# Two input slabs of a hybrid decoder trunk as split fp32r products, with the split spread over ScalarE and VectorE

## The reference, cut to what matters

```python
h = layer_norm(x, ln_in_g, ln_in_b)                  # x: 1 x 256 x 1024, float32
for l in range(2):
    p = h @ w_in[l]                                  # 1024 x 2560
    q, k = rotary(p[q columns]), rotary(p[k columns])     # 8 heads x 64 each
    v = p[v columns]
    y_att = moba_attention(q, k, v)                  # one block of 256: plain causal attention here
    y_sg = gelu(u) * (W_s layer_norm(gelu(v_sg)) + b)     # u, v_sg: 256 columns each
    y_cv = silu(layer_norm(depthwise_conv_31(a * sigmoid(g))))   # a, g: 256 columns each
    h = layer_norm(alpha * h + concat(y_att, y_sg, y_cv) @ w_out[l])
    h = layer_norm(alpha * h + moe(h))               # router, top-1 group of 4, top-2 of its 4 experts
```

## Time and profile before

| | |
|---|---|
| median of 3 runs | 721.97 us (721.77 to 723.27) |
| profiled execution | 721.64 us, span 719.8 us |
| mean granted TensorE clock | 0.987 |
| TensorE matmul busy | 670.3 us (93%) |
| VectorE, ScalarE, GpSimd busy | 281.1, 141.3, 67.9 us |
| chain that ended last | PE 72%, DMA 18%, DVE 7% |
| fp32 slab matmuls in the chain (L465) | 15% |
| read from memory | 239.1 MB |

### The profile page before, as it was taken

How to read it: one execution, slowest core, us unless ns; L and a number is a source line. 1 busy time by engine, 2 the same in 40 slices (tenths; PEclk the granted TensorE clock), 3 DMA queues, 4 the chain that set the end, 5 groups by cost and what they waited for, 6 DMA issues and landing times.

```text
span 719.8 us, 7383 instructions
## 1 busy us (share of the span) xinstructions
PE 670.3 (93%) x3039; PEld 329.5 (46%) x3039; DVE 281.1 (39%) x585; ACT 141.3 (20%) x280; POOL 67.9 (9%) x65
## 2 busy tenths in 40 slices
PE   7999999999999999987689999989999999998882
PEld 4645587543333543332375446856333445332331
DVE  4496767410333022130627936771120330321226
ACT  3102453231110211110121026523201113100100
POOL 1603000410000000000050210006000000000001
PEclk9999999999999999999979999999999999999997
DMA  8999636099999999999999641433999999999991
GB/s 282 341 388 413 270 118 234 5 374 405 421 422 421 421 421 421 421 421 421 396 387 404 266 163 67 158 128 151 372 422 422 421 421 421 422 420 422 421 407 66
DMA packets 48572, 240.72 MB, mean 334 GB/s; under 512 B 4428, under 2 KB 8852, under 8 KB 23956
## 3 DMA queue, kind: packets, MB, share of 16 engines
q1 hardware_dynamic: 47956, 238.06, 82.4%
q10 hardware_dynamic: 576, 2.10, 0.7%
HBM read 239.10 MB, written 1.05 MB: 334 GB/s over the span
## 4 chain that ended last, share of the span: by engine, by line
PE 72%; DMA 18%; DVE 7%; issue 1%; ACT 1%; POOL 0%; DVEq 0%; POOLq 0%; ACTq 0%
PE bank L544 22%; PE bank L465 15%; PE bank L563 12%; DMA ring<-in_w_up 9%; DMA ring<-in_w_gate 8%; PE bank L479 5%; PE bank L522 5%; PE bank L625 4%; PE bank L583 3%; PE bank L552 1%; PE bank L443 1%; PE bank L697 1%; DVE stats L1217 1%; DVE h L1210 1%; PE bank L688 1%
## 5 line engine op out<-in xcount | busy, mean ns | idle before, releaser
L544 PE MATMUL bank<-ring,xe 128*64 128x512 f32 x1024 | 226.0, 594 | 14.9 <-DMA ring<-in_w_up 7.9
L544 PEld LDWEIGHTS bank<-ring,xe 128*64 128x64 f32 x1024 | 71.7, 137 | 162.4 <-issue 136.1
L563 PE MATMUL bank<-ring,area_b 128*64 128x512 f32 x512 | 113.4, 595 | 1.6 <-DVE area_b L1231 1.6
L465 PE MATMUL bank<-ring,xT_area 128*128 128x512 f32 x256 | 111.3, 593 | 0.0
L1225 DVE TENSOR_TENSOR area_b<-area_b,bank 128x512 f32<-128x512 f32 x16 | 11.0, 687 | 253.7 <-PE bank L544 253.7
L465 PEld LDWEIGHTS bank<-ring,xT_area 128*128 128x128 f32 x256 | 48.1, 190 | 57.4 <-issue 57.4
L563 PEld LDWEIGHTS bank<-ring,area_b 128*64 128x64 f32 x512 | 35.2, 137 | 68.4 <-issue 64.0
L950 POOL TENSOR_TENSOR rstd<-var_eps,half_neg 128x1 f32<-128x1 f32 x18 | 11.7, 660 | 544.9 <-DVE var_eps L1037 544.9
L1245 DVE SCALAR_TENSOR_TENSOR y_lo<-bank,slot_gate,y_hi 128x512 fp32r<-128x512 f32 x32 | 24.0, 751 | 89.2 <-ACT y_hi L871 89.2
L1293 DVE SCALAR_TENSOR_TENSOR mix<-glu,tapsT,mix 128x256 f32<-128x256 f32 x120 | 47.7, 471 | 0.0
L871 ACT ACTIVATE y_hi<-bank,slot_gate 128x512 fp32r<-128x512 f32 x32 | 22.0, 687 | 98.1 <-PE bank L563 98.1
(11 more groups left out here) (159 smaller groups left out, 577.2 us busy)
## 6 DMA issues: line engine op xcount, KB each, us to landing
ring<-in_w_gate SPq DMA_DIRECT2D x32, 2048.0 KB, 22.8
ring<-in_w_up SPq DMA_DIRECT2D x32, 2048.0 KB, 23.8
ring<-in_w_down SPq DMA_DIRECT2D x32, 2048.0 KB, 24.5
ring<-in_w_in SPq DMA_DIRECT2D x9, 2048.0 KB, 20.4
ring<-in_w_out SPq DMA_DIRECT2D x4, 2048.0 KB, 21.0
ring<-in_w_in SPq DMA_DIRECT2D x2, 1024.0 KB, 7.1
h<-in_x SPq DMA_DIRECT2D x2, 512.0 KB, 4.1
ln_par<-in_ln_mix_g ACTq DMA_DIRECT2D x2, 512.0 KB, 7.5
```

Of the source, the lines that this page charges most:

```text
L465: mm = pe.matmul(dst[:, :], xT[:, c, b * P:(b + 1) * P], w[:, c, :], start=c == 0, stop=c == KC - 1)
L544: mm = pe.matmul(bank[2 + u % 2][e * SLOTS:(e + 1) * SLOTS, :], xe[:, k, at + e * SLOTS:at + (e + 1) * SLOTS], w[:, e, c, :], start=k == 0 ...
L563: mm = pe.matmul(bank[5 + n][e * SLOTS:(e + 1) * SLOTS, :], hidT[:, k, e * SLOTS:(e + 1) * SLOTS], w[:, e, c, n * BANK:(n + 1) * BANK], st ...
```

## The change

The q and k slabs are computed like w_out: each chunk of 128 contraction rows and each row block is three fp32r matmuls. The turned input gets a high part (ScalarE, two copies of 1024 columns) and a low part (VectorE, four subtractions of 512). Each of the 16 weight chunks gets a high part in one of seven buffers (ScalarE) and a low part, which is written over the chunk in the ring (VectorE). Seven chunks are split ahead of the sigmoid (ScalarE) and of the gated product (VectorE); the others on ScalarE behind it as buffers come free, and on VectorE one after every second pair of taps.

On TensorE sgu moves ahead of the turn of the convolution's result, and the first block of v (now into bank 5) ahead of the turns of q and k. ScalarE takes over the copies of the turned k and of the set-up parameters; its silu moves behind the copies of turned q and k, and its load of the next layer norm's rows behind the last high part. The first layer norm's rows are loaded between the halves of slab 0, and GpSimd applies them before it masks the spatial weights.

```diff
+IN_SPLITS = 7
+IN_CHUNKS = 2 * KC
...
+        xi_hi = nc.alloc_sbuf_tensor_at("xi_hi", [P, KC, SEQ], F32R, offset=uv_at)
+        xi_lo = nc.alloc_sbuf_tensor_at("xi_lo", [P, KC, SEQ], F32R, offset=area_b_at + 4096)
+        in_hi_at = [uv_at + 8192 + 2048 * i for i in range(4)] + [area_b_at + 2048, area_a_at + 6144, area_a_at + 10240]
...
             def load_setup():
-                sp.dma_start(ln_par[:, 0, :], bcast_row(ln_in_g, D)).then_inc(par_in, 16)
-                sp.dma_start(ln_par[:, 1, :], bcast_row(ln_in_b, D)).then_inc(par_in, 16)
...
                     sp.dma_start(dst[:, :, CV:], src[:, :, CV:]).then_inc(first_half_in, 16)
+                    sp.dma_start(ln_par[:, 0, :], bcast_row(ln_in_g, D)).then_inc(par_in, 16)
+                    sp.dma_start(ln_par[:, 1, :], bcast_row(ln_in_b, D)).then_inc(par_in, 16)
                     sp.dma_start(dst[:, :, 0:CV], src[:, :, 0:CV]).then_inc(landed[0], 16)
...
+            def in_product(l, i, b):
+                n, c = i // KC, i % KC
+                if i == 0:
+                    pe.wait_ge(xi_hi_ready, TB * l + b + 1)
+                    pe.wait_ge(xi_lo_ready, TB * l + b + 1)
+                if b == 0:
+                    pe.wait_ge(in_lo_ready, IN_CHUNKS * l + i + 1)
+                w_hi, w_lo = in_hi[i % IN_SPLITS][:, :], in_lo[(l * LAYER_UNITS + 1 + n) % RING][:, c * BANK:(c + 1) * BANK]
+                for k, (x, w) in enumerate(((xi_hi, w_hi), (xi_lo, w_hi), (xi_hi, w_lo))):
+                    mm = pe.matmul(bank[2 * n + b][:, :], x[:, c, b * P:(b + 1) * P], w,
+                                   start=c == 0 and k == 0, stop=c == KC - 1 and k == 2)
+                    if b == TB - 1 and k == 1:
+                        mm.then_inc(in_chunk_used, 1)
+                if b == TB - 1 and c == KC - 1:
+                    mm.then_inc(used, 1)
...
-                rows_slab(u0 + 1, (0, 1))
-                if l == 0:
-                    pe.wait_ge(setup_copied, 1)
-                rows_slab(u0 + 2, (2, 3))
+                for i in range(IN_CHUNKS):
+                    if l == 0 and i == KC:
+                        pe.wait_ge(setup_copied, 1)
+                    for b in range(TB):
+                        in_product(l, i, b)
+                rows_slab(u0 + 3, (6, 7))
...
-                rows_slab(u0 + 3, (6, 7))
+                block_slab(u0 + 4, 0, bank[5]).then_inc(v0_pe, 1)
...
-                pe.wait_ge(conv_ln_done, TB * (l + 1))
-                block_slab(u0 + 4, 0, bank[4]).then_inc(v0_pe, 1)
...
+                pe.wait_ge(conv_ln_done, TB * (l + 1))
                 pe.wait_ge(v_ready, TB * l + 1)
...
+            def in_x_high(l):
+                for b in range(TB):
+                    act.wait_ge(tr_dve, TR_DVE * l + b + 1)
+                    act.wait_ge(tr_act, TR_ACT * l + b + 1)
+                    act.activation(xi_hi[:, :, b * P:(b + 1) * P], xT[:, :, b * P:(b + 1) * P], ACT.Copy)\
+                       .then_inc(xi_hi_ready, 1)
+            def in_w_high(l, i):
+                n = l * LAYER_UNITS + 1 + i // KC
+                if i % KC == 0:
+                    act.wait_ge(landed[n % RING], 16 * (n // RING + 1))
+                if i >= IN_SPLITS:
+                    act.wait_ge(in_chunk_used, IN_CHUNKS * l + i - IN_SPLITS + 1)
+                act.activation(in_hi[i % IN_SPLITS][:, :], unit_at(n)[:, i % KC * BANK:(i % KC + 1) * BANK], ACT.Copy)\
+                   .then_inc(in_hi_ready, 1)
...
                 scaled_columns(3 * l, 2 * l, [(0, 0), (1, 0)])
+                in_x_high(l)
+                for i in range(IN_SPLITS):
+                    in_w_high(l, i)
                 act.wait_ge(used, l * LAYER_UNITS + 1)
                 act.activation(conv_sig, bank[5][:, :].rearrange("p (c t) -> p c t", c=CB), ACT.Sigmoid)\
                    .then_inc(sig_ready, 1)
+                if l == 0:
+                    act.wait_ge(setup_pe, DEPTH + 1)
...
+                    ins.then_inc(setup_copied, 1)
+                for i in range(IN_SPLITS, IN_CHUNKS):
+                    in_w_high(l, i)
                 next_params(ln_mix_g[l], ln_mix_b[l], 2 * TB * l + TB)
+                act.wait_ge(used, l * LAYER_UNITS + 4)
...
+                for b in range(TB):
+                    for i in range(2):
+                        act.wait_ge(qkT_pe, 4 * l + 2 * b + i + 1)
...
                 act.wait_ge(conv_ln_done, TB * (l + 1))
                 act.activation(mix[:, :, ATT + SG:D], mix[:, :, ATT + SG:D], ACT.Silu).then_inc(conv_out, 1)
...
+            def in_x_low(l):
+                for b in range(TB):
+                    dve.wait_ge(xi_hi_ready, TB * l + b + 1)
+                    for half in range(2):
+                        x = slice(4 * half, 4 * half + 4), slice(b * P, (b + 1) * P)
+                        ins = dve.tensor_tensor(xi_lo[:, x[0], x[1]], xT[:, x[0], x[1]],
+                                                xi_hi[:, x[0], x[1]].bitcast(F32), ALU.subtract)
+                    ins.then_inc(xi_lo_ready, 1)
+            def in_w_low(l, i):
+                dve.wait_ge(in_hi_ready, IN_CHUNKS * l + i + 1)
+                at, cols = (l * LAYER_UNITS + 1 + i // KC) % RING, slice(i % KC * BANK, (i % KC + 1) * BANK)
+                dve.tensor_tensor(in_lo[at][:, cols], ring[:, at, cols], in_hi[i % IN_SPLITS][:, :].bitcast(F32),
+                                  ALU.subtract).then_inc(in_lo_ready, 1)
...
                 scaled_columns(3 * l, 2 * l)
+                in_x_low(l)
+                for i in range(IN_SPLITS):
+                    in_w_low(l, i)
...
                         ins.then_inc(conv_step, 1)
+                    if k % 2 == 1 and IN_SPLITS + k // 2 < IN_CHUNKS:
+                        in_w_low(l, IN_SPLITS + k // 2)
...
-                for b in range(TB):
-                    dve.wait_ge(qkT_pe, 4 * l + 2 * b + 2)
-                    dve.tensor_copy(qkT[:, 1, :, b * P:(b + 1) * P],
-                                    bank[2 + b][:, :].rearrange("p (c t) -> p c t", c=4)).then_inc(qkT_dve, 1)
```

More of the change, by code:

```diff
@@ L106, in trunk @@
         ring = sb("ring", [RING, UNIT])
+        ring_at = nc.sbuf_base - 4 * RING * UNIT
         h = sb("h", [TB, D])
@@ L190, in trunk @@
                    for i in range(SPLITS)]
+        xi_hi = nc.alloc_sbuf_tensor_at("xi_hi", [P, KC, SEQ], F32R, offset=uv_at)
+        xi_lo = nc.alloc_sbuf_tensor_at("xi_lo", [P, KC, SEQ], F32R, offset=area_b_at + 4096)
+        in_hi_at = [uv_at + 8192 + 2048 * i for i in range(4)] + [area_b_at + 2048, area_a_at + 6144, area_a_at + 10240]
+        in_hi = [nc.alloc_sbuf_tensor_at(f"in_hi{i}", [P, BANK], F32R, offset=at) for i, at in enumerate(in_hi_at)]
+        in_slots = sorted({(l * LAYER_UNITS + 1 + n) % RING for l in range(DEPTH) for n in range(2)})
+        in_lo = {at: nc.alloc_sbuf_tensor_at(f"in_lo{at}", [P, UNIT], F32R, offset=ring_at + 4 * UNIT * at) for at in in_slots}
         xe = nc.alloc_sbuf_tensor_at("xe", [P, KC, GROUP * P], F32, offset=xT_at)
@@ L253, in trunk @@
         proj_pe = sem("proj_pe")
+        xi_hi_ready = sem("xi_hi_ready")
+        xi_lo_ready = sem("xi_lo_ready")
+        in_hi_ready = sem("in_hi_ready")
+        in_lo_ready = sem("in_lo_ready")
+        in_chunk_used = sem("in_chunk_used")
+        taps_copied = sem("taps_copied")
         x_hi_ready = sem("x_hi_ready")
@@ L881, in _ @@
                    .then_inc(sig_ready, 1)
+                if l == 0:
+                    act.wait_ge(setup_pe, DEPTH + 1)
+                    nt = DEPTH * TAPS + DEPTH
+                    act.activation(tapsT[:, :, :], bank[3][:, 0:CB * nt].rearrange("p (c k) -> p c k", c=CB), ACT.Copy)\
+                       .then_inc(taps_copied, 1)
+                    act.activation(sgbT[:, :], bank[3][:, 256:256 + DEPTH * GROUPS], ACT.Copy)
+                    for n in range(DEPTH):
+                        ins = act.activation(sgwT[:, n, :, :], bank[6 + n][:, :].rearrange("p (g t) -> p g t", g=GROUPS),
+                                             ACT.Copy)
+                    ins.then_inc(setup_copied, 1)
+                for i in range(IN_SPLITS, IN_CHUNKS):
+                    in_w_high(l, i)
                 next_params(ln_mix_g[l], ln_mix_b[l], 2 * TB * l + TB)
-                act.wait_ge(conv_ln_done, TB * (l + 1))
-                act.activation(mix[:, :, ATT + SG:D], mix[:, :, ATT + SG:D], ACT.Silu).then_inc(conv_out, 1)
                 act.wait_ge(used, l * LAYER_UNITS + 4)
@@ L973, in gain_and_shift @@
                 pool.tensor_tensor(h[:, b, :], h[:, b, :], ln_par[:, 1, :], ALU.add).then_inc(h_ready, 1)
+            pool.wait_ge(norm_ready, TB)
+            for b in range(TB):
+                gain_and_shift(b, 0)
+            pool.wait_ge(setup_in, 16 * 4)
+            pool.affine_select(out=sgw_rows, in_=sgw_rows, compare_op=ALU.is_ge, fill=0.0, base=0,
+                               pattern=[[0, DEPTH * GROUPS], [-1, P]], channel_multiplier=1).then_inc(sgw_masked, 1)
```

43 lines of the change are left out of this document (16 added, 27 removed).

## The result

| | before | changed |
|---|---|---|
| median, first comparison (4 runs each) | 721.87 us (720.44 to 723.27) | 714.11 us (713.15 to 715.77) |
| ratio, first comparison | | 0.9895, 95% interval 0.987 to 0.9919 |
| median, second comparison (11 and 6 runs) | 721.85 us | 714.76 us |
| ratio, second comparison | | 0.9901, 95% interval 0.9881 to 0.9921 |
| profiled execution (its span) | 721.64 us (719.8) | 713.42 us (711.6) |

The change makes the kernel faster by 7.8 us by the first medians and 7.1 by the second. 714.3 was forecast, within 711.3 to 717.8.

The account below looks back on a forecast made before the run. The prediction took VectorE's period of 2.19 us per chunk to set the end of q and k. Gains of 2.7 and 5.1 less 0.2 us, 7.6 together, gave 714.3 us as a median, range 711.3 to 717.8.

Parts of the forecast that it names:

- TensorE's rate: In the q and k slabs: each fp32r matmul takes 0.227 us, 21.8 us for the 96.
- The last chunk: End of q and k: chunk 15's six matmuls take 1.36 us after a hand-over of 0.05 us.
- Layer 1: Layer 1's q and k products: done at 404.2 instead of 409.3 us, a gain of 5.1 us.
- Layer 0: Layer 0's q and k products: k lands at 35.0, done at 53.0 against 55.7 us, a gain of 2.7 us.
- What hides what: Both mixers: sgu and half of v hide taps and rotation, with 4.4 and 5.1 us of cover for the rotation.
- Exponentials, 1.1 us later, at no cost: ScalarE's exponentials: ready about 0.2 us before the spatial matmuls instead of 1.3, so 1.1 us later, costing nothing.
- The input's low parts: VectorE before the taps: four subtractions for the turned input, each costing 0.60 us.
- The first layer norm's rows: Layer 0's slab 0: loading them earlier delays its second half 2.7 us at most, at no cost to the sigmoid.
- The table load: ScalarE before layer 0's sigmoid: a load costs 1.28 us, against about 2.66 by the skill page.
- Rival (a): Both layers' q and k: TensorE's own rate decides, not VectorE's subtractions; 710.6 us, chance 8%.
- Rival (b): Layer 0: k lands no earlier or the sigmoid later, gain 0.8 us or below; 716.2 to 717 us, chance 18%.
- Rival (c): Both mixers: TensorE's waits lower its granted clock, slowing the sgu slab behind; 724.6 us, chance 5%.

Follow-up runs that it names:

- e1: Changed kernel with one subtraction after every pair of taps instead of every second pair: 710.32 us, ratio 0.9839 to the kernel before.
- e2: Changed kernel with the next layer norm's parameter rows loaded ahead of ScalarE's last nine high parts again: 718.79 us, one run.
- e8: Changed kernel with only the sigmoid's table loaded earlier, ahead of ScalarE's high parts: 717.59 us, one run.
- e3: Changed kernel with sgu put back behind the turns of conv and half of v behind those of q and k: 735.44 us, one run.
- e4: Changed kernel with only half of v put back behind the turns of q and k: 720.3 us, one run.
- e6: Changed kernel with subtractions late among the taps, then one after every pair, and the sigmoid's table loaded ahead of ScalarE's high parts: 711.09 us, ratio 0.984.
- e5: Changed kernel with GpSimd's gain and shift held back until VectorE's subtractions (layer 1: through chunk 6) are done: 716.45 us, one run.
- e7: e6 with 22 filler matmuls added ahead of layer 1's turns to keep the clock up: 716.23 us.

## Why the prediction was right, and where its terms were off

- **The bound.** Right. VectorE's period was forecast at 2.19 us and is 2.19; the chain shows it in both layers, and in e1 the bound is gone and q and k run at TensorE's rate.
- **TensorE's rate.** Right: 0.227 us a product, 21.79 for the 96 in e1.
- **The last chunk.** Mis-sized. 1.36 us were forecast; a chunk that begins after an idle moment takes 1.66, and its first matmul shows 0.50 us where the others show 0.40. The hand-over is 0.04 (0.05 forecast), but the subtraction behind VectorE's last wait counts with its 0.69 and not with 0.60. That is 0.4 us in each layer.
- **Layer 1.** q and k take 22.71 us against 27.47: 4.8 where 5.1 was forecast, for the reason above.
- **Layer 0.** The term that was mis-sized most: 2.7 us forecast, 1.3 to 1.7 measured. The mis-sized step is "1.05 MB at the 387 GB/s of a busy window are 2.7 us; I take three quarters of it, 2.0": k landed at 35.41 and 35.91 and not at 35.0. Counted from slab 0's start it lands at 23.1 us in both profiles, where it was 24.15, 24.19 and 24.27 in three of the kernel before: 1.0 to 1.2 us earlier. With the last chunk's 0.4 that is 1.2 to 1.4 us less. The lower bound of 0.8 with k at 36.9 was too high as well: e2, where k lands late, gains 0.35 at most. The mechanism was the right one: e2 moves k and the end of q and k by the same amount, and e8 moves the sigmoid by 1.35 us and the end of q and k not at all.
- **What hides what.** Right. e3 and e4 uncover it: the waits of 1.93 and 1.33 us in e4 are 6.87 us of half of v less the covers of 4.4 and 5.1 that were forecast, to within 0.5 and 0.4. The scores' wait for ScalarE's copies of the turned q and k costs 0.16 us a layer (0.1 forecast): in TensorE's timeline the sixteen turns take 1.91 us to the next matmul, and 1.75 in the kernel before.
- **Exponentials, 1.1 us later, at no cost.** They start at 80.69, 0.4 us ahead of the spatial product at 81.11 (0.2 forecast), so 0.8 later, and nothing behind them waits.
- **The input's low parts.** Mis-sized without a cost: 4 x 0.60 were taken, and beside GpSimd they took 6.81 and 6.56 us, ahead of the taps in both layers.
- **The first layer norm's rows.** Right. Slab 0 of layer 0 takes 14.05 us before and after, and GpSimd's four products end at 24.4 in place of 30.3.
- **A shorter mixer is worth what it is shorter by.** Right: ahead of the experts the transfers stand still as before (0 GB/s from 127 to 141, and 1 from 472 to 487), and the expert stages keep their length.
- **The table load.** 1.28 was taken; it shows 1.28, the sigmoid starts 0.02 us behind it, and in e6, without it there, 1.35 us earlier. The Trainium skill (ScalarE: Activation LUTs, What ACT_TABLE_LOAD costs) would have it at about 2.66; in this kernel the measurement decides against it.
- **Rival (a), TensorE's rate decides (710.6).** Not in this kernel, but it is what e1 makes of it: 710.32.
- **Rival (b), layer 0 gives nothing.** Half of it came: the layer gave 1.3 to 1.7, between the forecast's 2.7 and its 0.8. e2 is its case in full.
- **Rival (c), the clock falls.** Refuted for idle moments of 0.54 us in 2.2: the granted clock is 1.00 in every window from q's first matmul to the last of w_out in both layers. It is real at 8.66 us, as e3 shows. (Its 714.3 + 10.2 are 724.5, not 724.6.) The section of the Trainium skill that spoke for it (TensorE: Matmul & The Clock Gate, A second HAM failure mode: psum-queue depth-cycling) isn't borne out by this pattern of waits.
- **The sum.** 7.6 was forecast; the steps themselves gave 5.7 to 6.1. The rest of the medians' 7.1 to 7.8 came from outside the steps, in the profiles for the most part from the clock at the start of layer 1. That 714.3 lies within 0.5 us of both medians is luck.

## What to carry to other kernels

When work that one engine must prepare is woven into another task of that engine, compute the period of the weave and compare it with what the consumer eats per piece: 2.19 against 1.36 us here, and one line that makes it 1.40 was worth 4 us more than the change alone. When the fast engine gets faster, list what its long stage used to cover; here it was the taps and the rotation, and without sgu and half of v moved ahead the gain of 7 us would have been a loss of 13. And compare stretches between fixed instructions in two or three profiles of both kernels before giving a difference of 2 us a cause.

## What the runs showed of the hardware that was not expected

- VectorE's subtraction of two SBUF operands and GpSimd's product hold each other up: 0.69 us alone, up to 2.84 beside GpSimd, and GpSimd's 2.35 become 2.80. The Trainium skill (SBUF — State Buffer, Who interferes with whom) says that such a pair shares ports that one instruction holds for its whole length; e5 agrees, for kept apart they take 0.69 and 2.35 again.
- After a stretch of idle time TensorE's granted clock came back after different times in one and the same program: the 64 matmuls of layer 1's slab 0 took 15.60, 17.07 and 15.52 us in three profiles of the kernel before. In the changed kernel they took 14.05 twice, and 17.11 in e8.
- Between the experts' last matmul and the next layer's first one TensorE stands for 5.57 us even for instructions without data to wait for (e7). A branch stands there in its program; what takes this time wasn't tried.
